# Attention softmax taken two heads at a time, its last multiplication moved to GpSimd, and one product's weight halves made a tile earlier

## The reference

```python
s = scores * 64 ** -0.5 + bias          # a query's logits, a sink logit beside them in the second block
p = softmax(s)                           # exp(s - max) / sum
o = p @ v
```

## Time and profile before

| what | value |
|---|---|
| median of 3 runs | 2094.41 us |
| the profiled execution's own time | 2094.94 us |
| its span, first to last instruction | 2093.1 us |
| TensorE matmul / weight load busy | 96% / 84% of the span |
| VectorE, ScalarE, GpSimd busy | 61%, 45%, 21% |
| mean granted TensorE clock | 0.988 |
| first block's units | 290.64 to 347.41 us |
| layer 0's units | 964.80 to 1050.63 us |
| layer 1's units | 1777.55 to 1835.75 us |

### The profile page before, as it was taken

The page is one execution under the profiler, slowest core; times in us unless marked ns, Lnnn a source line. Parts: engine busy times, 40 slices in busy tenths (PEclk is TensorE's granted clock), DMA queues, the critical chain, the costliest instruction groups (busy, mean ns, idle before and its releaser), DMA issues.

```text
span 2093.1 us, 30363 instructions
## 1 busy us (share of the span) xinstructions
PE 2007.8 (96%) x12246; PEld 1756.3 (84%) x12246; DVE 1267.9 (61%) x1962; ACT 944.5 (45%) x1493; POOL 433.4 (21%) x270
## 2 busy tenths in 40 slices
PE   7999899899989999999999999999989899998999
PEld 6899887899978888787688788888878898697999
DVE  5678797778855863543863583354365946776410
ACT  5444445555446333323653542243265453655643
POOL 1201000000000000000044554555500000002887
PEclk9999999999999999999999999999999999999999
DMA  7987461566722112211023344466522333144554
GB/s 254 273 295 263 159 234 41 180 223 229 264 91 95 60 48 91 91 61 61 1 81 111 109 150 143 149 202 202 181 88 94 101 121 111 51 141 142 182 191 151
DMA packets 84636, 299.22 MB, mean 143 GB/s; under 512 B 9993, under 2 KB 13201, under 8 KB 84113
## 3 DMA queue, kind: packets, MB, share of 16 engines
q1 hardware_dynamic: 64512, 231.76, 32.3%
q0 software_dynamic: 17280, 60.95, 9.1%
q10 hardware_dynamic: 2704, 4.57, 0.6%
HBM read 296.18 MB, written 4.11 MB: 143 GB/s over the span
## 4 chain that ended last, share of the span: by engine, by line
PE 79%; DVE 10%; ACT 5%; issue 3%; DMA 3%; ACTq 0%; POOL 0%; DVEq 0%; POOLq 0%
PE ps L458 21%; PE ps L453 21%; PE ps L456 21%; DVE wl L436 3%; DMA wr<-wstream 2%; ACT wh L420 2%; PE ps L1601 1%; PE ps L538 1%; PE ps L982 1%; PE ps L984 1%; PE ps L987 1%; PE ps L1042 1%; PE ps L1059 1%; PE ps L1082 1%; PE ps L1039 1%
## 5 line engine op out<-in xcount | busy, mean ns | idle before, releaser
L453 PE MATMUL ps<-HH,wh 128*128 128x256 f32 (+1 forms) x2336 | 766.8, 328 | 22.8 <-ACT HH L1320 10.7
L458 PE MATMUL ps<-HH,wl 128*128 128x256 f32 (+1 forms) x2336 | 753.5, 323 | 7.2 <-DVE wl L436 6.0
L456 PE MATMUL ps<-HL,wh 128*128 128x256 f32 (+1 forms) x2336 | 752.1, 322 | 0.5 <-DVE HL L1334 0.4
L420 ACT ACTIVATE wh<-wr 128x1024 fp32r<-128x1024 f32 x440 | 461.2, 1053 | 387.1 <-PE ps L458 333.5
L436 POOL TENSOR_TENSOR wl<-wr,wh 128x1024 fp32r<-128x1024 f32 x143 | 355.8, 2493 | 993.5 <-ACT wh L420 992.6
L436 DVE TENSOR_TENSOR wl<-wr,wh 128x1024 fp32r<-128x1024 f32 x297 | 361.8, 1227 | 246.8 <-ACT wh L420 244.4
L453 PEld LDWEIGHTS ps<-HH,wh 128*128 128x128 f32 x2336 | 449.1, 192 | 67.3 <-issue 28.7
L458 PEld LDWEIGHTS ps<-HH,wl 128*128 128x128 f32 x2336 | 448.9, 192 | 43.1 <-DVE wl L436 9.3
L456 PEld LDWEIGHTS ps<-HL,wh 128*128 128x128 f32 x2336 | 449.2, 192 | 36.9 <-issue 2.4
L458 PE MATMUL ps<-HIDH,wl 128*128 128x512 f32 (+1 forms) x512 | 173.1, 338 | 0.0
L453 PE MATMUL ps<-HIDH,wh 128*128 128x512 f32 (+1 forms) x512 | 172.8, 338 | 0.0
(11 more groups left out here) (255 smaller groups left out, 2604.1 us busy)
## 6 DMA issues: line engine op xcount, KB each, us to landing
wr<-wstream SPq DMA_DIRECT2D x440, 512.0 KB, 3.3
WM<-wmod POOLq DMA_DIRECT2D x68, 512.0 KB, 4.0
X<-wmod POOLq DMA_DIRECT2D x28, 512.0 KB, 5.4
NAB<-naskew POOLq DMA_DIRECT2D x16, 128.0 KB, 12.6
dilskew<-lines POOLq DMA_DIRECT2D x1, 2048.0 KB, 20.8
DILB<-dilskew POOLq DMA_DIRECT2D x2, 1024.0 KB, 13.5
COND<-cond ACTq DMA_DIRECT2D x2, 1024.0 KB, 5.9
CT<-consts POOLq DMA_DIRECT2D x1, 1216.0 KB, 9.5
```

The lines of the kernel that those rows point to most:

```text
L420: ins = e.activation(self.WH[i % NSPL][:, :], self.WR[n % NRAW][:, :], ACT.Copy)
L453: e.matmul(out, wh, xh, start=i == 0, stop=False)
L456: e.matmul(out, wh, xl, start=False, stop=False)
L458: ins = e.matmul(out, wl, xh, start=False, stop=i == n_k - 1)
```

## The change

- **Pairs.** `pe_units`, `act_units` and `dve_units` take two units a step. The two have `off` 0 and `off` 64; for that `layer_units` puts the two key heads next to each other. TensorE gives out the scores of both alternately, matmul by matmul, and so the values (`pe_scores`, `pe_values_of`). A step is now: transposes of pair t-1, scores of pair t+1, fill, values of pair t-2.
- **Multiplication on GpSimd.** The multiplication by the reciprocal leaves VectorE (1176) and stands in GpSimd's stream as `pool_units`, after `pool_bias_loads`, after the issues of the modulation weights 28 to 47 of layer 0, and before the last low halves of layer 1.
- **VectorE's order.** With A and B the two units of a pair, a step is for `b1` and `c`: reciprocal of A's sum, scores of the next A, reciprocal of B's sum, scores of the next B, then both maxima of the next pair; for `x`: both sums, both scores, both maxima. The sink is added by `tensor_scalar`.
- **Heads of the first block.** Squares are taken two tiles at a time, with other counts of empty steps; the high halves of heads 2 and 3 move behind the loop.
- **Output product of layer 1.** The high half of tile d+1 is made before the square of tile d, and the low half of tile d+1 after X of tile d.

```diff
 def layer_units(l):
     out = []
     for j in range(4):
-        for kv in range(2):
-            for a in range(2):
+        for a in range(2):
+            for kv in range(2):
                 out.append(Unit(("x", l, j, kv, a), "x", 1, 64 * kv, j, a, j + 4 * kv, ("xo", l, j),
                                 kv == 0 and a == 0, kv == 1 and a == 1))
...
+    def pe_scores(self, e, w, pair, S, qk):
...
+        parts = [self.score_parts(u) for u in pair]
+        for i in range(len(parts[0])):
+            for u, part in zip(pair, parts):
+                a, b, queries, keys = part[i]
+                ins = e.matmul(self.aux.item(("s", u.key))[:, a:b], queries, keys, start=True, stop=True)
+                if i == len(part) - 1:
+                    ins.then_inc(*self.c("u_score").mark(u.key))
+
+    def pe_values_of(self, e, w, pair, P, v_there):
...
+        parts = [self.value_parts(u) for u in pair]
+        for i in range(4):
+            for u, part in zip(pair, parts):
+                at, values, c, start, stop = part[i]
+                ins = e.matmul(b[u.off:u.off + 64, at:at + 128], values, P.item(u.key)[:, c:c + 128], start=start, stop=stop)
+                if i == 3:
+                    ins.then_inc(*self.c("u_pv").mark(u.key))
+                    P.release(u.key, self.c("u_pv"), u.key)
+
     def pe_units(self, e, w, units, rings, qk, v_there, fill):
+        pairs = list(zip(units[::2], units[1::2]))
+        n = len(pairs)
+        for t in range(-1, n + 2):
+            for u in pairs[t - 1] if 1 <= t <= n else ():
...
+            if t + 1 < n:
+                self.pe_scores(e, w, pairs[t + 1], S, qk)
             fill()
+            if t >= 2:
+                self.pe_values_of(e, w, pairs[t - 2], P, v_there)
...
     def act_units(self, e, w, units, rings, l, s_free, fill):
+        for t in range(-1, n + 2):
+            for u in pairs[t] if 0 <= t < n else ():
+                self.act_unit_exp(e, w, u, S, l)
+            for u in pairs[t + 1] if t + 1 < n and pairs[t + 1][0].kind == "x" else ():
...
+            for u in pairs[t - 1] if 1 <= t <= n else ():
...
             fill()
...
     def dve_units(self, e, w, units, rings, l, s_free, out, fill):
+        for t in range(-1, n + 2):
+            after = pairs[t + 1] if t + 1 < n else ()
+            both = not after or after[0].kind == "x"
+            for i in range(2):
+                if 0 <= t < n:
+                    self.dve_unit_sum(e, w, pairs[t][i])
+                if not both:
+                    self.dve_unit_scores(e, w, after[i], S, s_free)
+            for u in after if both else ():
+                self.dve_unit_scores(e, w, u, S, s_free)
+            for u in after:
+                self.dve_unit_max(e, w, u, S, l)
             fill()
...
+    def pool_units(self, e, w, units, rings):
+        for u in units:
+            rows, st = u.rows, self.ST[:, self.st.item(u.key), :]
+            sv = rings[0].item(u.key)[:, :].rearrange("p (r k) -> p r k", r=rows)
+            w.wait_ge(*self.c("u_inv").at(u.key))
+            ins = e.tensor_tensor(sv, sv, bc(st[:, 4:4 + rows], 2, 512 // rows), ALU.mult)
+            ins.then_inc(*self.c("u_p").mark(u.key))
+            self.st.release(u.key, self.c("u_p"), u.key)
...
     def act_add_out(self, e, w, key, ks, T, squares):
+        ahead = 1 if key == ("out", 1, 0) else 0
         for d in range(8):
-            self.make_high(e, w, *self.steps(key + (d,), ks))
+            for n in range(d + ahead if d else 0, min(d + ahead + 1, 8)):
+                self.make_high(e, w, *self.steps(key + (n,), ks))
             if squares:
                 self.act_square(e, w, key, d, self.X[:, d, 0:T], [self.c("x_new").at(key + (d, T // 256 - 1))])
...
     def dve_add_out(self, e, w, key, l, T, mod_i, squares, mod):
+        by_dve = key == ("out", 1, 0)
+        if by_dve:
+            self.make_low(e, w, "lo_dve", (key + (0,), 0))
         for d in range(8):
-            if key == ("out", 1, 0):
-                self.make_low(e, w, "lo_dve", (k, 0))
...
+            if by_dve and d < 7:
+                self.make_low(e, w, "lo_dve", (key + (d + 1,), 0))
...
     def pool(self, e):
         self.pool_bias_loads(e, w)
+        self.pool_units(e, w, block1_units(), self.unit_rings(1))
...
         for ch in range(MOD_A, 48):
             self.pool_mod(e, w, 0, 1, ch)
+        self.pool_units(e, w, layer_units(0), self.unit_rings(2))
...
+        self.pool_units(e, w, layer_units(1), self.unit_rings(2))
         self.make_low(e, w, "lo_pool", *self.steps(("ff2", 1, 0, 7), range(32)))
```

More of the change, by code:

```diff
@@ L1021, in unit_sink, with score_parts @@
         return self.vec("attn_sink_2", 8 * l + u.head)
+    def score_parts(self, u):
+        rows, j = slice(u.off, u.off + 64), u.j
+        if u.kind == "x":
+            return [(0, 512, self.Q2[rows, j, 128 * u.a:128 * u.a + 128], self.K2[rows, :])]
+        if u.kind == "b1":
+            return [(256 * a, 256 * a + 256, self.QT[rows, j, 128 * a:128 * a + 128], self.KT[rows, j, :]) for a in range(2)]
+        return [(256 * a, 256 * a + 256, self.Q2[rows, j, 256 + 128 * a:384 + 128 * a], self.K2[rows, 256:512])
+                for a in range(2)]
@@ new lines, in value_parts @@
+    def value_parts(self, u):
+        if u.kind == "x":
+            return [(128 * u.a, self.V2[:, c, u.off:u.off + 64], 128 * c, c == 0, c == 3) for c in range(4)]
+        if u.kind == "b1":
+            return [(128 * a, self.VR[:, k, 64 * u.head:64 * u.head + 64], 256 * a + 128 * k, k == 0, k == 1)
+                    for a in range(2) for k in range(2)]
+        return [(128 * a, self.V2[:, 2 + c, u.off:u.off + 64], 256 * a + 128 * c, c == 0, c == 1)
+                for a in range(2) for c in range(2)]
@@ new lines, in pe_scores @@
+    def pe_scores(self, e, w, pair, S, qk):
+        for u in pair:
+            S.take(u.key)
+            self.st.take(u.key)
+            self.aux.take(("s", u.key))
+            for x in self.aux.before(("s", u.key)) + qk(u):
+                w.wait_ge(*x)
+        parts = [self.score_parts(u) for u in pair]
[5 more added lines that the diff above has]
+                    ins.then_inc(*self.c("u_score").mark(u.key))
@@ new lines, in pe_values_of @@
+    def pe_values_of(self, e, w, pair, P, v_there):
+        group = pair[0].group
+        if pair[0].first:
+            self.main.take(group)
+            for x in self.main.before(group):
+                w.wait_ge(*x)
+        b = self.main.item(group)
+        for u in pair:
+            w.wait_ge(*self.c("u_pt").at(u.key))
+            for x in v_there(u):
+                w.wait_ge(*x)
+        parts = [self.value_parts(u) for u in pair]
[6 more added lines that the diff above has]
+                    P.release(u.key, self.c("u_pv"), u.key)
@@ new lines, in dve_unit_sum @@
+    def dve_unit_sum(self, e, w, u):
+        st = self.ST[:, self.st.item(u.key), :]
+        den = st[:, 4:4 + u.rows]
+        w.wait_ge(*self.c("u_exp").at(u.key))
+        if u.kind != "b1":
+            for i in range(u.rows):
+                ins = e.tensor_scalar(den[:, i:i + 1], den[:, i:i + 1], st[:, 6 + i:7 + i], None, ALU.add)
+            ins.then_inc(*self.c("u_den").mark(u.key))
+            w.wait_ge(*self.c("u_den").at(u.key))
+        e.reciprocal(den, den).then_inc(*self.c("u_inv").mark(u.key))
@@ L1179, in dve_units @@
             fill()
-            if t >= 3 and units[t - 3].final:
-                u = units[t - 3]
+            if t >= 2 and pairs[t - 2][1].final:
+                u = pairs[t - 2][1]
                 w.wait_ge(*self.c("u_pv").at(u.key))
```

239 lines of the change are left out of this document (84 added, 155 removed).

## The result

The changed kernel takes 2041.64 us (median of 4 runs, 2041.20 to 2047.00), the kernel before 2095.11 in the same measurement: ratio 0.9751, interval 0.9733 to 0.9770, 53.5 us less. A second measurement of the same two gave 0.9762 (0.9747 to 0.9777), 50.5 us less.

A forecast was written before the change was run, and what follows sets the result against it. TensorE was taken to bound the units, then a chain through GpSimd after the change. Gains of 12.6 + 15.9 + 11.4 + 3.7 = 43.6 us, less 4.3, took 39.3 off 2094.94: 2056 us, range 2043 to 2072.

The forecast's parts named there:

- TensorE's part: TensorE's work for a pair of units: transposes 1.02, scores 1.55, values 1.3, together 3.9 us against 5.30 before.
- only A's second can lie beside B's first: Pair's scores: two instructions per fp32 product, going A A B B, so row halves overlap only partly; scores taken as 1.55 us.
- The rival that had both halves overlap in full: Units: TensorE stays the bound, GpSimd's chain fits below 3.9 us; 8 us more gained, 2048 us; chance 0.20.
- the deductions of the forecast: Losses subtracted from the summed gains: 3 us for GpSimd meeting VectorE, 1 for first multiplication, 0.3 for heads' pacing; 4.3 us.
- The chain that becomes the limit: Uncovered unit steps: scores, softmax, GpSimd's multiplications, transposes span two steps; (6.2 + 0.5 + 1.55) / 2 = 4.13 us a pair.
- they pass: Work per pair of VectorE 3.4 to 3.5 us, ScalarE 3.3, GpSimd 2.5 was said to fit within the step.
- the forecast's own signs: Units: score starts 4.1 to 4.2 us apart, GpSimd ending transposes' idle time; mechanism wrong if TensorE waits in filled steps.
- the first rival: Units: TensorE stays the bound with both halves overlapping fully; sign 3.9 us between score starts, 2048 us, chance 0.20.
- The stretches: Three stretches of units: first block 44.2 us for 56.8, layer 0 69.9 for 85.8, layer 1 46.8 for 58.2.
- Output product: Layer 1's output product: tiles 2.87 us apart instead of 3.45, seven intervals of 0.58, with a later start 3.7 us saved.
- What is taken off: Whole kernel: 4.3 us deducted from the gains, 3 of them for GpSimd and VectorE blocking each other (0 to 12).
- the 39.3: Whole kernel: net gain forecast in us, 43.6 saved less 4.3 taken off.

The follow-up runs named there:

- p4_divide_8: Changed kernel with four buffers p in the first block and layer 1, and GpSimd multiplying only 8 columns of each row; median 2037.6 us.
- divide_8_columns: Changed kernel with GpSimd multiplying only 8 of each row's columns, nothing else moved; median 2043.6 us.
- values_in_turn: Changed kernel with TensorE giving out A's four value products, then B's four, instead of alternating; median 2045.1 us.
- deeper: Changed kernel with scores first, four buffers p, six score buffers and sets of sums in first block and layer 1, reordered VectorE and ScalarE; median 2055.9 us.

## Why the prediction fell short

- *TensorE's part.* Forecast 1.02 + 1.55 + 1.3 = 3.87; measured 1.02 + 1.06 + 1.03 = 3.11, which is a whole step where nothing waits (p4_divide_8). The step "only A's second can lie beside B's first" failed. Scores of A and B run side by side from their first instruction (x4 in 1.13, 1.98 without halves), values too. The rival that had both halves overlap in full was right in this; its 2048 was still too high, as it kept the deductions of the forecast.
- *The chain that becomes the limit.* Forecast 6.2 us and 4.13 a step; measured 6.3 us and 3.91. The chain's own terms were about right (GpSimd's multiplication 1.04 for 1.25); with the measured scores its sum gives (6.3 + 0.5 + 1.06) / 2 = 3.93, so 1.55 for 1.06 is the mis-sized term in 4.13. But the chain isn't what ends the steady step. The step "they pass", said of the rest, failed: I had called the `aux` banks not binding and never looked at the two buffers `p`, and of ScalarE and VectorE I had compared work (3.3, 3.5) with the step, not their loop, which is 3.93. By the forecast's own signs the mechanism is wrong: the transposes' idle time in steady steps is ended by ScalarE, not GpSimd, and TensorE waits for the copy in the filled step with values too (6.90, and 6.10 with four buffers `p`). A step of 3.9 was to speak for the first rival, yet TensorE stands 0.68 us in it. That the size came out near is luck: three limits lie together. For `c` 4.7 was forecast, 4.52 measured.
- *The stretches.* Forecast 44.2, 69.9 and 46.8; measured 45.3, 68.2 and 45.6. The first block came out 1.1 longer than forecast; four buffers `p` took 0.8 off its filled step with values and 1.8 off its last steps, so the wait for the copy is more than enough for that. Together 41.7 us for 39.9.
- *Output product.* Forecast 3.7, measured 6.8. The tiles are 2.80 us apart at the end (2.87 forecast); the term left out is VectorE's lag of 4.4 us behind the product, which the forecast kept as it was: its first two intervals shrank to 1.5 and 2.2 us where 2.87 was forecast for all.
- *What is taken off.* 4.3 us were forecast, nothing was lost. GpSimd's 56 multiplications took 1030 to 1045 ns, the first too. Contention was there once, and VectorE paid it, 0.60 us for 0.42:

```profile
1788.03 2.04 POOL L1210 TENSOR_TENSOR s<-s,ST 128x512 f32<-128x512 f32 x2 [1.54 <-DVE ST L1178]
...
1789.74 0.60 DVE L2118 TENSOR_TENSOR HL<-FR,HH 128x256 fp32r<-128x256 f32 x1 [0.92 <-ACT HH L2112]
```

  VectorE's operation of two SBUF inputs began inside GpSimd's. The Trainium skill, "SBUF — State Buffer", Who interferes with whom, has whoever issues second blocked for the first's instruction. This agrees in who is slowed; a full block isn't shown, as the two lay 0.32 us side by side and VectorE lost 0.18. Such a meeting is rare here by the order of the units: VectorE's other two-input operations beside the multiplications are its scalings of scores from PSUM, which took 0.42 and 0.68 us there as elsewhere. Here I had charged for the earlier trace rows, which come from a stretch where VectorE streams such operations.

Of the 10 us by which the gains seen in the spans (41.7 + 6.3 + 1.3 = 49.3) exceed the 39.3, 4.3 are that deduction, 2.6 the product, 1.8 the units, 1.3 the time between layer 0 and 1. That time goes with the clock. Over all kernels it is 725.3 to 726.1 us where 10.2 to 13.7 of them are at the lower level, and 726.6 to 728.0 where 16.2 to 18.7 are; before the change it was 726.9 with 17.1, in the changed kernel 725.6 with 10.2. So this gain isn't shown to be the change's. The last 1 to 4 us, up to 50.5 and 53.5, are inside what executions of one kernel differ by.

## What to carry to other kernels

Count waits that come back to the same engine (TensorE's values, a copy, TensorE's transposes) as part of its row, and list the buffers that each copy needs, the small rings too. Work out each loop of two engines by adding its rows once around, for "busy less than the step" clears no engine. When an edit removes a limit and nothing moves, take the next one away as well before the theory is dropped: here three stood at 3.9 us. And before a few microseconds are read as an edit's effect, compare the granted clock of the stretches: divide_8_columns hid half of its gain behind it.

## What the runs showed of the hardware

- 64-row scores on both row halves, and 64-column values on both column halves, cost for two units about what they cost for one (1.06 and 1.03 us a pair, 1.05 and 1.02 for one unit before). The Trainium skill, "TensorEngine Tiling (Array Packing)", Key Properties, says that different tiles can load weights and multiply in parallel; the traces now show it for rows also, from the first instruction on. The values lie side by side in part even if the stream doesn't alternate (1.58 for 1.09), and then B's first starts ahead of instructions of A that were given out before it (values_in_turn).
- GpSimd's 128 x 512 multiplication with a broadcast factor takes 1.04 us, less than half of the 1024-wide subtraction's 2.41.
- Idle time of TensorE can be followed by the lower clock, and need not be. In deeper TensorE was busy 1.18 of 3.20 us at a granted clock of 1.00; 2 us later the clock was 0.51 for 3.2 us, and 1.00 again behind it (the column before the last two). In the last 12.4 us of the changed kernel's layer 0 TensorE was busy 7.8, and the clock stayed at 1.00. At the lower level sixteen value products last 1.98 us for 1.09 (divide_8_columns).

```profile
299.30:302.50 3.20, 1.18 (x9) 0.72 (x9) 3.17 (x8) 2.08 (x8) 2.14 (x2) 1.00 0.30 109
302.50:304.60 2.10, 1.73 (x11) 1.44 (x12) 1.80 (x7) 1.03 (x2) 1.07 (x2) 0.96 0.70 244
304.70:307.90 3.20, 3.20 (x9) 2.43 (x9) 1.34 (x1) 2.97 (x10) 1.72 (x2) 0.51 0.03 8
308.00:312.00 4.00, 4.00 (x25) 2.97 (x25) 2.33 (x5) 1.85 (x3) 0.00 (x0) 1.00 0.36 133
```
